# Two routers that read raw rows: the reciprocal root is applied to the logits, and the last tiles are turned elsewhere in the order

## The reference

```python
h = rmsnorm(x, p['norm2']) * (1 + sc2) + sh2
x = x + g2 * expert_choice_ffn(h, p['w_router'], p['w_gate'], p['w_up'], p['w_down'])
...
aff = jax.nn.softmax(jnp.einsum('td,de->te', t, w_router).astype(jnp.float32), axis=-1)
g, idx = lax.top_k(aff.T, cap)
xe = t[idx]
```

## Time and profile before

| What | us |
|---|---|
| Runs of the kernel before, median of 3 | 2191.89 |
| lowest and highest of them | 2178.64, 2196.59 |
| the profiled execution | 2183.08 |
| its span, first to last instruction | 2181.3 |
| PE busy, share of the span | 2028.1, 93% |
| DVE busy | 862.9, 40% |
| ACT busy | 469.6, 22% |
| mean granted clock of TensorE | 0.961 of full |

### The profile page before, as it was taken

How to read it: one execution, slowest core, us unless ns; L and a number is a source line. 1 busy time by engine, 2 the same in 40 slices (tenths; PEclk the granted TensorE clock), 3 DMA queues, 4 the chain that set the end, 5 groups by cost and what they waited for, 6 DMA issues and landing times. The chain is left out here.

```text
span 2181.3 us, 27642 instructions
## 1 busy us (share of the span) xinstructions
PE 2028.1 (93%) x11531; PEld 1433.6 (66%) x11531; DVE 862.9 (40%) x1810; ACT 469.6 (22%) x928; POOL 155.0 (7%) x149
## 2 busy tenths in 40 slices
PE   5999999979999999999799999995997499999998
PEld 2776777755666665443587878783443387878785
DVE  2245344455666664337322222222647522222221
ACT  1222222126566663113100000001232100000000
POOL 0000000000000000000111111111000101111110
PEclk9999999989999999999899999997898599999999
DMA  9201111038444422844777878766221787878782
GB/s 352 96 25 49 41 44 37 30 98 265 181 177 173 151 100 85 297 145 152 282 242 259 303 259 303 250 223 226 88 104 58 280 321 251 302 260 303 259 284 61
DMA packets 159149, 404.29 MB, mean 185 GB/s; under 512 B 12617, under 2 KB 30736, under 8 KB 152882
## 3 DMA queue, kind: packets, MB, share of 16 engines
q1 hardware_dynamic: 142370, 344.30, 43.8%
q0 software_dynamic: 16656, 58.24, 9.3%
HBM read 339.46 MB, written 63.05 MB: 185 GB/s over the span
## 5 line engine op out<-in xcount | busy, mean ns | idle before, releaser
L1983 PE MATMUL experts_gu<-experts_h_t,shared_w_gate 128*128 128x160 f32 x2048 | 303.2, 302 | 4.1 <-issue 4.1
L1983 PEld LDWEIGHTS experts_gu<-experts_h_t,shared_w_gate 128*128 128x128 f32 x2048 | 289.4, 192 | 19.2 <-issue 19.2
L1983 PE MATMUL experts_gu<-experts_h_t,shared_w_up 128*128 128x160 f32 x2048 | 299.9, 300 | 0.0
L1983 PEld LDWEIGHTS experts_gu<-experts_h_t,shared_w_up 128*128 128x128 f32 x2048 | 286.1, 191 | 0.0
L2059 DVE TENSOR_TENSOR experts_hid<-experts_act,experts_gu 128x160 f32<-128x160 f32 x128 | 41.2, 322 | 479.5 <-ACT experts_act L2048 479.5
L2007 PE MATMUL experts_dn<-shared_w_down,experts_hid 128*128 128x512 f32 x512 | 225.8, 594 | 0.0
L523 PE MATMUL proj_cv<-proj_h_t,proj_w_in 128*128 128x256 f32 x960 | 213.9, 381 | 2.6 <-DVE proj_h_t L720 2.6
L2048 ACT ACTIVATE experts_act<-experts_gu 128x160 f32<-128x160 f32 x128 | 38.8, 303 | 813.6 <-PE experts_gu L1983 813.6
L523 PEld LDWEIGHTS proj_cv<-proj_h_t,proj_w_in 128*128 128x128 f32 x960 | 182.6, 192 | 29.2 <-issue 4.7
L2007 PEld LDWEIGHTS experts_dn<-shared_w_down,experts_hid 128*128 128x128 f32 x512 | 94.7, 190 | 113.8 <-issue 113.8
L1008 PE MATMUL attn_sc<-attn_keys_s,attn_q_s 96*128 96x512 f32 (+1 forms) x384 | 154.6, 539 | 3.8 <-DVE attn_pr_t L1141 2.8
(11 more groups left out here) (413 smaller groups left out, 2110.7 us busy)
## 6 DMA issues: line engine op xcount, KB each, us to landing
shared_w_gate<-w_gate_l SPq DMA_DIRECT2D x32, 2048.0 KB, 9.4
shared_w_up<-w_up_l SPq DMA_DIRECT2D x32, 2048.0 KB, 17.1
shared_w_down<-w_down_l SPq DMA_DIRECT2D x32, 2048.0 KB, 22.0
attn_w_mod<-w_mod_l SPq DMA_DIRECT2D x40, 1024.0 KB, 6.4
proj_w_in<-w_in_l SPq DMA_DIRECT2D x3, 2048.0 KB, 20.4
proj_x<-x POOLq DMA_DIRECT2D x10, 512.0 KB, 3.9
shared_w_down<-x SPq DMA_DIRECT2D x10, 512.0 KB, 4.5
layer_room_a<-w_mod_l SPq DMA_DIRECT2D x4, 1024.0 KB, 10.1
```

The costliest lines, as they stand in the source:

```text
L1983: last = pe.matmul(gu[j % 2][:, m * SLOTS:(m + 1) * SLOTS], w[u][:, k, j * P:(j + 1) * P], h_t[u][:, k, :], start=(k == 0), stop=(k == KD ...
```

## The change

Both routers transpose and multiply the raw residual rows; the logits are multiplied by each token's reciprocal root, and the bias added, on DVE after the parts are summed (`Choice.normalise`). The bias is made for all 128 partitions, with the shift column broadcast as the stationary operand. In layer 0's stage the reciprocal roots get a buffer for all tiles, the waits for `xh` move from `turn` to `residual`, and the ends of all streams are reordered. In layer 1's stage the last latent pair is turned and routed between the context products.

```diff
@@ class Choice
-                last = pe.matmul(self.banks[0][0:NE, c:c + 1], self.w_r[:, k, :], self.per.shift2[self.layer][:, c, k:k + 1], start=(k == 0), stop=(k == KD - 1))
+                last = pe.matmul(self.banks[0][:, c * NE:(c + 1) * NE], self.per.shift2[self.layer][:, c, k:k + 1].broadcast_to([P, P]), self.w_r[:, k, :],
+                                 start=(k == 0), stop=(k == KD - 1))
...
-        act.activation(self.lg_sb[u][:, 0:n], self.banks[u][:, 0:n], ACT.Identity, bias=self.bias[:, c:c + 1]).then_inc(self.lg_kept[u], 1)
+        act.activation(self.lg_sb[u][:, 0:n], self.banks[u][:, 0:n], ACT.Copy).then_inc(self.lg_kept[u], 1)
...
+    def normalise(self, dve, ch, c, rstd):
...
+        dve.wait_ge(self.bias_kept, 1)
+        bias = self.bias[:, c, :].unsqueeze(1).broadcast_to([P, rstd.shape[1], NE])
+        ch.link(dve.tensor_tensor(self.logits[c], self.logits[c], self.spread(c, rstd), ALU.mult))
+        ch.link(dve.tensor_tensor(self.logits[c], self.logits[c], bias, ALU.add))
@@ output_and_choice, PE
-                    pe.wait_ge(xh_ready, m + 1)
+                    pe.wait_ge(y_ready, m + 1)
...
                 for m in range(1, NT):
+                    if m == NT - 1:
+                        choice.turn_affinities(pe, 1)
                     product(m, 0, 0, KD)
...
                     else:
-                        choice.turn_affinities(pe, 1)
                         product(m, 1, 0, 4)
...
-                mixing_weights(0, 8)
+                mixing_weights(0, 3)
                 turn(NT - 1)
+                mixing_weights(3, 5)
                 router(NT - 1)
                 choice.turn_batch(pe, 2)
-                mixing_weights(8, 11)
+                mixing_weights(5, 9)
                 choice.turn_affinities(pe, 0)
-                mixing_weights(11, N_W)
+                mixing_weights(9, N_W)
@@ output_and_choice, ACT
                 square(ST)
+                turned_both(ST)
                 scaled(ST)
-                turned_both(ST)
-                mixing_weights_kept(0, 4)
+                mixing_weights_kept(0, 3)
                 square(ST + 1)
-                mixing_weights_kept(4, 8)
+                ch.link(act.activation(ms[0][:], eps[:], ACT.Exp))
+                turned_both(ST + 1)
+                mixing_weights_kept(3, 5)
+                choice.keep_batch(act, 2)
+                mixing_weights_kept(5, 7)
+                choice.exponentials(act, 0)
                 scaled(ST + 1)
-                turned_both(ST + 1)
-                choice.keep_batch(act, 2)
-                choice.exponentials(act, 0)
-                mixing_weights_kept(8, N_W)
+                mixing_weights_kept(7, N_W)
@@ output_and_choice, DVE (residual also waits for the turned tile m - 2 and for xh m - 2)
                     residual(m)
-                    normalise(m)
                     fold(m)
                     turned(m)
+                    normalise(m)
...
+                choice.normalise(dve, ch, 1, rt_s)
                 choice.shift(dve, ch, 1)
+                choice.divide(dve, ch, 1)
                 residual(ST)
-                choice.divide(dve, ch, 1)
+                choice.keep_affinities(dve, ch, 1)
+                choice.rounds(dve, ch, 0, 2)
                 invert(ST)
-                choice.keep_affinities(dve, ch, 1)
-                choice.rounds(dve, ch, 0, 6)
                 residual(ST + 1)
-                choice.rounds(dve, ch, 6, 8)
+                choice.rounds(dve, ch, 2, 4)
                 invert(ST + 1)
-                choice.rounds(dve, ch, 8, 12)
+                choice.rounds(dve, ch, 4, 6)
                 choice.add_parts(dve, 2)
+                dve.wait_ge(inverted, PT)
+                choice.normalise(dve, ch, 0, rt_p)
                 choice.shift(dve, ch, 0)
-                choice.rounds(dve, ch, 12, 13)
+                choice.rounds(dve, ch, 6, 7)
                 choice.divide(dve, ch, 0)
-                choice.rounds(dve, ch, 13, 14)
+                choice.rounds(dve, ch, 7, 14)
                 choice.keep_affinities(dve, ch, 0)
@@ fourier_and_choice, PE (turn reads x_a, x_b and waits for y_ready)
+                i = PAIRS - 2
                 for m, results in enumerate(context_products()):
                     product(bank(m), results)
-                i = PAIRS - 2
-                turn(i, 0)
-                turn(i, 1)
-                router(i, 0)
-                router(i, 1)
+                    if m:
+                        if m < 3:
+                            turn(i, m - 1)
+                        if m > 1:
+                            router(i, m - 2)
@@ fourier_and_choice, ACT
-                turned(PAIRS - 2)
+                ch.link(act.activation(ends[:, 0, 0:1], eps[:], ACT.Exp))
                 choice.keep_batch(act, 0)
                 choice.keep_batch(act, 1)
                 choice.exponentials(act, 1)
                 choice.keep_near(act)
+                normalised(PAIRS - 2)
                 ch.link(act.activation(rt_y[:, PAIRS - 1, 0:1], eps[:], ACT.Sqrt))
                 square(PAIRS - 1)
-                normalised(PAIRS - 1)
+                ch.link(act.activation(ends[:, 0, 0:1], eps[:], ACT.Exp))
...
                 choice.exponentials(act, 0)
+                normalised(PAIRS - 1)
@@ fourier_and_choice, DVE
                 move(0, 2)
+                turned_both(last, 0)
+                move(2, 3)
+                turned_both(last, 1)
+                move(3, N_CONTEXT)
                 root(last)
-                move(2, N_CONTEXT)
-                turned(last)
                 choice.add_parts(dve, 0)
                 choice.add_parts(dve, 1)
+                dve.wait_ge(root_ready, PAIRS - 1)
+                choice.normalise(dve, ch, 1, rt_y[:, 0:PAIRS - 1, :].rearrange("p i s -> p (i s)"))
                 choice.shift(dve, ch, 1)
...
                 choice.add_parts(dve, 2)
+                dve.wait_ge(root_ready, PAIRS)
+                choice.normalise(dve, ch, 0, rt_y[:, PAIRS - 1, :])
                 choice.shift(dve, ch, 0)
```

More of the change, by code:

```diff
@@ L1294, in prepare_tables @@
     def prepare_tables(self, dve):
-        for tile in (self.bias, self.pads[0], self.pads[1], self.aff):
+        for tile in (self.pads[0], self.pads[1], self.aff):
             dve.memset(tile[:], 0.0)
@@ L1436, in output_and_choice @@
         y_t = [weights.down[3][:, 0, :], s.sb("y1", [P, D])[:]]
-        ms, rt = [s.sb(f"ms{u}", [P, 1]) for u in range(2)], [s.sb(f"rt{u}", [P, 1]) for u in range(2)]
+        ms = [s.sb(f"ms{u}", [P, 1]) for u in range(2)]
+        rt_s, rt_p = s.sb("rt_s", [P, ST]), s.sb("rt_p", [P, PT])
         eps = s.sb("eps", [P, 1])
@@ L1629, in square @@
                     ch.link(act.activation(junk, y_t[u][:], ACT.Square, accum_out=ms[u][:]))
-                    act.activation(rt[u][:], ms[u][:], ACT.Sqrt, bias=eps[:], scale=1.0 / D).then_inc(ms_ready, 1)
+                    act.activation(rt(m), ms[u][:], ACT.Sqrt, bias=eps[:], scale=1.0 / D).then_inc(ms_ready, 1)
                 def turned(m):
@@ L1694, in residual @@
                     wait(dve, ms_ready, m - 1)
+                    wait(dve, tp_full, 2 * m - 2)
+                    wait(dve, xh_ready, m - 1)
                     dve.tensor_tensor(y_t[u][:], acc[u][:], gate[:, condition(m), :], ALU.mult).then_inc(gated, 1)
```

38 lines of the change are left out of this document (22 added, 16 removed).

## The result

| What | us |
|---|---|
| Runs of the changed kernel, median of 22 | 2197.72 (2188.91 to 2207.83) |
| Runs of the kernel before beside them, median of 22 | 2182.89 (2177.87 to 2196.59) |
| ratio, with its 95% interval | 1.0060 (1.0044 to 1.0076) |
| forecast (range) | 2205.4 (2193 to 2217), within 1% |
| the profiled execution of the changed kernel | 2193.15, span 2191.4, mean clock 0.964 |

What follows compares the result with a forecast made beforehand. PE, busy 93% of the span, was taken to bound the kernel, with PE and DVE balanced at layer 0's end. 2.6 + 2.6 + 1.2 + 1.2 + 4.8 + 0.6 + 0.5 = 13.5 us gave 2205.4 us, range 2193 to 2217.

Steps and rivals of the forecast that it cites:

- The bias: Both router stages: 32 instructions with a 128-wide stationary operand at 0.110 us, +2.6 us on PE each; bounds 0 and 3.9.
- The clock behind the bias: Products behind the bias, both stages: PE may fall to 1.2 GHz; 1.2 us taken twice, bounds 0 and 3.4.
- The end of layer 0's stage: DVE waits before `residual(9)`, rounds queue behind it, and the experts start at 1061.3 against 1056.48: +4.8 us, bounds +2.5 and +8.
- PE's wait for the affinities: Layer 0, before `product(9, 0)`: PE stands from 993.68 to 995.2 waiting for DVE, 1.5 us.
- DVE's hole: Layer 0, before `residual(9)`: DVE stands from 1002.8 to 1010.4 waiting for the end of `product(9, 1)`, 7.6 us.
- PE in that stage: End of layer 0's stage: PE loses its gaps and reaches the lists near 1041.5 instead of 1045.35, a gain with no taker.
- PE waiting 8 to 9 us for the lists: Sign to look for in the trace at the end of layer 0's stage: PE idle 8 to 9 us before the lists.
- The loop of layer 0: Layer 0's tile loop: no term of its own; the bias step said DVE, ACT and the loads run behind PE there.
- The experts' start in layer 0: First 14 us of layer 0's experts: less clock granted after a longer idle PE, +0.6 us; bounds 0 and 1.3.
- The end of layer 1's stage: Layer 1: about 0.5 us of gaps around turning fall away, `normalise` costs 0.64 and 0.5; net +0.5 us, bounds -5.1 and +1.5.
- The -5.1 set as a bound: End of layer 1's stage: lower bound if the new order keeps full clock, half of 10.2 us of work.
- the first expert's weights are issued some 3 us later: Layer 1: shows only if they land after the first products' operands are ready, some 6 us behind the barrier.

Runs made afterwards that it cites:

- Experiment 2: Changed kernel with layer 0's loop running `normalise(m)` ahead of `fold(m)` and `turned(m)` again, so rows are stored early: 2196.68 us, ratio 1.0047 to the kernel before.
- Experiment 4: Changed kernel with the last normalised rows of layer 1's stage made before the exp: 2194.30 us, ratio 1.0035 to the kernel before.
- Experiment 3: Changed kernel with five search rounds instead of two ahead of `residual(9)` in layer 0: 2192.77 us, ratio 1.0033 to the kernel before.
- experiment 5: Changed kernel with bias by one product, rows stored early in layer 0, three more rounds before `residual(9)`, layer 1's last rows before exp: 2178.42 us, ratio 0.9976.
- experiment 8: Experiment 5 with layer 1's context products in one piece again, the last latent pair turned and routed behind them: 2181.11 us, ratio 0.9985 to the kernel before.
- experiment 6: Experiment 5 with the second expert's 2 MB of down weights loaded some 10 us earlier, before the last tile's store: 2175.55 us, ratio 0.9965 to the kernel before.
- 1: Changed kernel with the bias summed over its eight blocks on DVE, then one matmul with ones: 2190.97 us, ratio 1.0019 to the kernel before.
- experiment 7: Kernel before with the 32 wide bias instructions added in both stages, their result unused: 2203.55 us (six runs), ratio 1.0082 to the kernel before.

## Why the prediction came out right, step by step

The class and the range were right, and so were the bias and the hole at the end of layer 0's stage, the two largest terms. That the sum came within 1 us is luck. Two delays were missed, 3.6 us in layer 0's loop and most of 3.6 at the end of layer 1's stage; what made up for them is smaller losses than forecast elsewhere and, in the profiled pair, 5.0 us by which the unchanged code ran faster.

**The bias: right.** 32 x 0.110 from the earlier trace rows against 3.49 us measured; the experiment that takes it away gives 3.35 us in each stage back. The Trainium skill ("TensorE: Matmul & The Clock Gate", Back-to-back issue gap) states about 81 ns for each, for a stream with 128 columns; by it the bias would have taken an estimated 2.6 us. The trace, 109 ns with 16 moving columns in float32, does not agree.

**The clock behind the bias: right as a possibility, twice 1.2 taken as its mean.** Measured either 0 (profiled execution, 1.00 granted around 868) or 3.4 in layer 0 and 1.7 in layer 1 (experiments 2 and 4). It fell in four of the five traces that have the wide products in layer 0, in three of the five in layer 1, and in none of the five without them. It is a matter of the execution; the bounds 0 and 3.4 held it. What decides whether it falls is not shown.

**The end of layer 0's stage: right.** PE's wait for the affinities: forecast 1.5, measured 1.38, or 1.54 by the starts of rows. DVE's hole: 7.6 and 7.75. The list to the experts: 10.9 and 10.7. In all +4.8 against 1.54 + 3.50 - 1.09 = +4.0. Experiment 3 shows that the hole carries it.

**PE in that stage: wrong, without effect.** "PE itself loses its gaps and would reach the lists near 1041.5" failed: `middle_weights` ended at 1050.03, and the sign "PE waiting 8 to 9 us for the lists" failed with it, at 2.25. I took PE's rows of before and only subtracted gaps; the load of 2 MB that SP issues at 1029.88 against POOL's small stores, which ACT and then PE wait for, was not in the step, nor the half clock behind that wait. With DVE last, it cost nothing; in experiments 3, 5 and 8 PE was the last to arrive, by 1.8, 0.7 and 3.9 us.

**The loop of layer 0: missed.** The change moves `normalise(m)` behind `turned(m)`, and the step that says what stands behind such a move was not worked out; the text says only that loads run behind PE. Measured: 2.09 us of waiting and 1.70 at half clock, +3.6 against the kernel before, which lost 0.3 there too. Experiment 2 takes it away. SP's queue carries a tile's store, the experts' weights and the next operands in one order, so what is late at its head is late at its end.

**The experts' start in layer 0:** forecast +0.6, bounds 0 and 1.3. The first 14 us were granted 0.58 against 0.65, 0.07 x 14 = 1.0, within the bounds. The rule behind the step, that a PE which idled longer is granted less afterwards, is not borne out: in layer 1 PE stood 13.32 us ahead of the experts against 9.73 before, and its first 14 us were granted 0.85 against 0.56.

**The end of layer 1's stage: mis-sized and by a wrong step.** Net +0.5 was forecast. To the last list it was -1.3. DVE's second sum of parts came 3.2 us earlier behind the first context product where 0.6 was forecast, because the products and turning had the full clock and turning no longer waits for ACT's rows. With half the clock the same code took 2.9 us more in experiment 6, so the -1.3 holds for this execution and not for all. 1.9 of the 3.2 went again up to the last list, where 1.1 was forecast for `normalise`. The -5.1 set as a bound took all 10.2 us of the work for half clock. Only the turning was at half nearly all along; at full clock the products took 5.08 us and the two turnings 1.1 each (experiment 8), 3 us less. Behind the list it was +3.6, and there the text had "the first expert's weights are issued some 3 us later", which "would show only if they landed after the first products' operands are ready". They were issued 4.0 us later against the last list, so the size was about right, and the reasoning was not: what showed was not their landing but their traffic in the way of POOL's fetch (8.9 us for 5.3). Experiment 4 shows it by taking it away, and this is the step that failed most plainly. The 2.9 us that the experts of layer 1 gained (452.16 for 455.03) are no effect of the change that the runs bear out: their first 14 us were granted 0.85 of the clock, against 0.56 before, but with the same late fetch experiments 2 and 3 had 455.13 and 453.69, and 1 had 452.07.

In sum, for the profiled pair: bias +5.2 as forecast; clock behind it 0 for 2.4; end of layer 0 +4.0 for 4.8; the missed loop +3.6 for 0; the end of layer 1 and its experts -0.6 for 0.5; +1.7 in the experts of layer 0 and the start of layer 1's stage for 0.6; and -3.8 by which this execution came sooner through the unchanged code ahead of the first bias. That makes 10.1. The runs, 13.0 us apart by the ratio, needn't carry the terms of the unchanged code, and the low clock behind the biases may be in some of them; how these share the 13.0 is not shown.

The 2205.4 us itself stood on a median of before of three runs, 2191.89, "8.8 above the profiled execution". With 22 runs that median is 2182.89, 0.2 below the profiled execution, and 13.5 above it is 2196.4. So the absolute figure was 7.7 us too high for a reason that has nothing to do with the change.

## What to carry to other kernels

An instruction stream that issues stores, large weight loads and small operands in one order turned a store that was 3 us late into a wait of 2 us for another transfer; when what a store waits for moves, follow the queue to the next small transfer behind it. Ahead of a wait on another engine's product, put as much independent work as the wait is long (here three more rounds), and then look at which engine comes last: before the change the two ends were within 1 us of each other. Ahead of trusting a stretch of one trace, compare the unchanged code in it: here one stretch of the same code took 67.45 us in one execution and 70.38 in another. A product whose stationary operand is 128 wide costs 0.11 us for each instruction with 16 moving columns as with one; sum on an idle engine first and multiply once (0.14 us in place of 3.49).

## What the runs showed of the hardware that was not expected

In experiment 7 PE was granted 1.2 GHz for 30 us while it was busy 28.6 of them, at the mixing weights; in the kernel before the same work had 0.91 granted from 1030 to 1040 and 1.00 from 1040 to 1045. The same code at layer 1's context products had the full clock in experiment 5 and half of it in experiment 6, and the last list came 2.9 us later for it. A float32 weight load with 16 moving columns is 0.109 us at full clock, and 0.126 and 0.158 over the 32 of them where the clock fell meanwhile (4.02 and 5.06 us). An indirect fetch went from 5.3 to 8.9 us when the weight loads ahead of it were issued 4 us closer to it, though it is small beside them and in another queue. The exp table load took 1.28 us with the next instruction 0.02 behind it, at its new place too (1020.57 to 1021.87), against the 2.66 us with a drain that the Trainium skill ("ScalarE: Activation LUTs", What ACT_TABLE_LOAD costs) states.
